# Latent attention in a two-block network: raw latents are projected, their norm becomes a column on the scores, and four heads rotate in one tile

## The reference

```python
cq, ckv, k_rope = _split(h @ w_in, (256, 128, 32))
q = (_rms_norm(cq, q_norm) @ w_uq).reshape(b, s, 16, 64 + 32)
q_nope, q_rope = q[..., :64], _rope(q[..., 64:], cos_m, sin_m)
k_rope = _rope(k_rope[:, :, None, :], cos_m, sin_m)[:, :, 0]
kv = (_rms_norm(ckv, kv_norm) @ w_ukv).reshape(b, s, 16, 64 + 64)
k_nope, v = kv[..., :64], kv[..., 64:]
sc = (q_nope . k_nope + q_rope . k_rope) * 96 ** -0.5      # causal softmax, times v, then @ w_out
```

## Time and profile before

| | us |
|---|---|
| median of 3 runs (3462.76 to 3471.7) | 3462.96 |
| profiled execution, its own time | 3462.46 |
| its span, first to last instruction | 3460.6 |
| TensorE busy | 3307.8 (96% of the span) |
| VectorE, ScalarE, GpSimd busy | 1969.4, 1264.1, 169.9 |

### The profile page before, as it was taken

One profiled execution on the slowest core, in us unless ns is written; L12 is line 12 of the kernel. 1 busy time (PEld: TensorE's weight loads), 2 busy tenths in 40 slices (PEclk: granted clock), 3 DMA queues, 4 the chain that ended last, 5 costly groups with the idle time before them and its releaser, 6 DMA issues.

```text
span 3460.6 us, 44062 instructions
## 1 busy us (share of the span) xinstructions
PE 3307.8 (96%) x16249; PEld 2737.8 (79%) x16249; DVE 1969.4 (57%) x2749; ACT 1264.1 (37%) x1953; POOL 169.9 (5%) x162
## 2 busy tenths in 40 slices
PE   7999998899999999998999999998999999889999
PEld 6888786788888788885587888898788887868887
DVE  6765534555764567555646545697555464555543
ACT  3222311454222322233344223565434343443332
POOL 0000002000000000001210000231000001000000
PEclk9999996799999999998899999999999999999999
DMA  5543233003553355322014543454333320023332
GB/s 176 169 134 97 89 98 62 1 1 105 164 154 94 94 172 164 97 81 71 7 50 135 167 123 97 128 159 137 101 97 97 101 93 25 1 73 97 97 104 67
DMA packets 389691, 344.21 MB, mean 99 GB/s; under 512 B 11392, under 2 KB 343485, under 8 KB 389565
## 3 DMA queue, kind: packets, MB, share of 16 engines
q1 hardware_dynamic: 389565, 342.52, 33.1%
HBM read 340.38 MB, written 2.10 MB: 99 GB/s over the span
## 4 chain that ended last, share of the span: by engine, by line
PE 86%; DVE 8%; ACT 3%; issue 2%; SPq 1%; POOL 0%; DMA 0%; ACTq 0%; DVEq 0%; POOLq 0%
PE ps L907 25%; PE ps L909 25%; PE ps L908 25%; PE ps L994 4%; DVE w_lo L1566 2%; PE ps L983 2%; PE ps L971 1%; ACT w_hi L1553 1%; PE ps L1157 1%; DVE rstd L2198 0%; PE ps L1139 0%; DVE q_mla L2592 0%; PE ps L1146 0%; SPq L855 0%; DVE t L2691 0%
## 5 line engine op out<-in xcount | busy, mean ns | idle before, releaser
L907 PE MATMUL ps<-a_hi,w_hi 128*128 128x512 f32 (+1 forms) x2936 | 1114.4, 380 | 43.1 <-DVE w_lo L1566 18.1
L908 PE MATMUL ps<-a_lo,w_hi 128*128 128x512 f32 (+1 forms) x2936 | 1106.9, 377 | 0.0
L909 PE MATMUL ps<-a_hi,w_lo 128*128 128x512 f32 (+1 forms) x2936 | 1106.7, 377 | 0.0
L1566 DVE TENSOR_TENSOR w_lo<-w_raw,w_hi 128x1024 fp32r<-128x1024 f32 (+1 forms) x532 | 646.2, 1238 | 249.3 <-ACT w_hi L1553 246.3
L1553 ACT ACTIVATE w_hi<-w_raw 128x1024 fp32r<-128x1024 f32 (+1 forms) x532 | 548.6, 1044 | 355.1 <-PE ps L909 345.9
L907 PEld LDWEIGHTS ps<-a_hi,w_hi 128*128 128x128 f32 x2936 | 556.5, 190 | 152.6 <-issue 39.7
L908 PEld LDWEIGHTS ps<-a_lo,w_hi 128*128 128x128 f32 x2936 | 556.7, 190 | 101.6 <-issue 2.0
L909 PEld LDWEIGHTS ps<-a_hi,w_lo 128*128 128x128 f32 x2936 | 556.0, 189 | 101.4
L907 PE MATMUL ps<-hs_hi,w_hi 128*128 128x512 f32 x1056 | 411.5, 390 | 10.6 <-DVE hs_lo L2660 10.6
L908 PE MATMUL ps<-hs_lo,w_hi 128*128 128x512 f32 x1056 | 410.9, 389 | 0.0
L909 PE MATMUL ps<-hs_hi,w_lo 128*128 128x512 f32 x1056 | 410.8, 389 | 0.0
(11 more groups left out here) (359 smaller groups left out, 3357.6 us busy)
## 6 DMA issues: line engine op xcount, KB each, us to landing
w_raw<-in_ffn_w_up SPq DMA_DIRECT2D x220, 512.0 KB, 4.8
w_raw<-in_ffn_w_down SPq DMA_DIRECT2D x154, 512.0 KB, 3.6
ada_raw<-in_ada_w SPq DMA_DIRECT2D x96, 512.0 KB, 4.0
w_raw<-in_ffn_w_gate SPq DMA_DIRECT2D x88, 512.0 KB, 4.9
w_raw<-in_ev_w_in SPq DMA_DIRECT2D x20, 512.0 KB, 3.7
w_raw<-in_attn_w_qkv SPq DMA_DIRECT2D x12, 512.0 KB, 3.8
w_raw<-in_ev_w_out SPq DMA_DIRECT2D x8, 512.0 KB, 4.3
w_raw<-in_mla_w_out SPq DMA_DIRECT2D x8, 512.0 KB, 3.6
```

Of the source, the lines that this page charges most:

```text
L907: mm(dst, hi, rhi, start=start, stop=False)
L908: mm(dst, hi, rlo, start=False, stop=False)
L909: return mm(dst, lo, rhi, start=False, stop=stop)
L1566: nc.vector.tensor_tensor(w_lo[:, s, 0:width], w_raw[:, s, 0:width], w_hi[:, s, 0:width].bitcast(F32), ALU.subtract).then_inc(lo_made.sem, 1)
```

## The change

What it does, all within this phase:

- The query latents are no longer normed. ScalarE multiplies the raw sums by the gain straight out of `ps` into `c_hi`, VectorE forms `c_lo` from `ps` too. The product of both norms' inverses, one number per token, is computed as four columns `q_rstd`, from the squares of the raw latents and the input's sum of squares, and enters as the scale of the instruction that adds the mask to the scores. The key-value latent is still normed, with one reciprocal of a sum that includes the input's.
- The last chunk of the latents is multiplied bank by bank, after the feature sum, so that the banks finish one after another.
- The weights of the queries are regrouped as they are split (`parted`): the rotary columns of four heads form one 128-column tile, plain columns of two heads another. Twelve products of six instructions replace sixteen. The keys of two heads form one tile, eight products of three instructions in place of sixteen; the values' columns lie together.
- The rotation works on `q_rope`, four heads of 32 rows in one 128-row tile: four swaps, each with three vector operations, interleaved with the projections. DMAs copy the rotated rows to the heads' `q_mla` (16 copies of 64 KB) and the rotated key to all heads (4 copies of 256 KB in place of GpSimd's copy). They stand in SyncE's queue ahead of six of the eight chunks of `w_out`. The attention waits for `rope_in`.

The diff, cut to what the prediction speaks of (removed code stands in the listing above):

```diff
-    rotation(part("mla_swap"), part("mla_cos"), part("mla_sin"), [(64, 16, pos * inverse(500000.0, 32))])
+    rotation(part("mla_swap"), part("mla_cos"), part("mla_sin"), 
+             [(first, 16, pos * inverse(500000.0, 32)) for first in range(0, P, 32)])
...
+        q_rope = arena("q_rope", [P, 4, SEQ], F32, 81920)
...
+            grouped.update({ph.first + c: (64, 32) for c in range(4, 8)})
+            grouped.update({ph.first + c: (64, 64) for c in range(8, 10)})
+            for signal in rope_in:
+                signal.plan(16 * 4)
             heads = [dict(q=(q_mla[0:96, h, :],), k=(k_mla[0:96, h, :],), v=lambda kb, h=h: v_mla[:, kb, h * HD:h * HD + HD],
-                          out=o_mla[:, :, h * HD:h * HD + HD], gate=None, need=None) for h in range(16)]
+                          out=o_mla[:, :, h * HD:h * HD + HD], gate=None, need=None, rope=rope_in[h // 4],
+                          scale=lambda c: q_rstd[:, c:c + 1]) for h in range(16)]
...
+                    for k in range(2):
+                        chunk(b + 10 + k, w["mla_w_out"][0][k * P:(k + 1) * P, :])
+                    for i in (0, 1, 2, 4, 3):
+                        sp.wait_ge(rd_s.sem, ph.rd0 + {0: 1, 1: 2, 2: 3, 4: 4, 3: 5}[i])
+                        for a in range(4):
+                            if i == 4:
+                                sp.dma_start(k_mla[64:96, 4 * a:4 * a + 4, :],
+                                             F_mla[64:96, 3, :].unsqueeze(1).to_broadcast([32, 4, SEQ])).then_inc(rope_in[i].sem, 16)
+                            else:
+                                sp.dma_start(q_mla[64:96, 4 * i + a, :], q_rope[32 * a:32 * a + 32, i, :]).then_inc(rope_in[i].sem, 16)
+                    for k in range(2, KT):
...
+                    if c == 0 and head.get("rope") is not None:
+                        pe.wait_ge(rope_in[4].sem, 16 * 4)
+                        pe.wait_ge(head["rope"].sem, 16 * 4)
...
+                    fold_ada(ph.before, 5, taken=False)
+                    w_ready(b + 3)
+                    pe.wait_ge(a_lo_s.sem, ph.al0 + KT)
+                    for t in range(4):
+                        for kk in range(2):
+                            last = latent(3, t, kk)
+                        last.then_inc(cm_s.sem if t < 3 else w_used.sem, 1)
...
+                    def query(columns, i, bank):
+                        for kk in range(2):
+                            last = three(ps[:, bank, :], columns(w_hi, i, kk), columns(w_lo, i, kk), c_hi[:, kk, :], c_lo[:, kk, :],
+                                         kk == 0, kk == 1)
+                        return last
...
+                    def query_swap(i, bank):
+                        evicted(3 * i + 1)
+                        if i == 0:
+                            pe.wait_ge(tab_s.sem, ph.tab0 + 64)
+                        mm(ps[:, bank, :], swap_mla[:, :], q_rope[:, i, :], start=True, stop=True).then_inc(rp_s.sem, 1)
...
+                    w_ready(b + 4)
+                    pe.wait_ge(a_lo_s.sem, n2.alo0 + 2)
+                    query(rope_columns, 0, 6).then_inc(cm_s.sem, 1)
+                    query(plain_columns, 0, 7).then_inc(cm_s.sem, 1)
+                    pe.wait_ge(sq_s.sem, n2.sq0 + 1)
+                    query(plain_columns, 1, 0).then_inc(w_used.sem, 1)
                     pe.wait_ge(root_s.sem, ph.root0 + 1)
...
+                    pe.wait_ge(sum_s.sem, n2.sum0 + 1)
+                    pe.wait_ge(sq_s.sem, n2.sq0 + 3)
+                    mm(ps[:, 4, :], ones[:, :], t1[:, :], start=True, stop=False)
+                    mm(ps[:, 4, :], ones[:, :], sq_sum[:, :], start=False, stop=True).then_inc(ss_s.sem, 1)
+                    pe.wait_ge(trc_s.sem, ph.before.trc0 + 1)
+                    for c in range(4):
+                        for i, part in enumerate((F_mla[:, 0, :], F_mla[:, 1, :], sq_sum[:, :])):
+                            last = mm(ps[:, 5, c:c + 1], part[:, c * P:(c + 1) * P], ones[:, 0:1], start=i == 0, stop=i == 2)
+                    last.then_inc(ss_s.sem, 1)
+                    w_ready(b + 5)
+                    query(rope_columns, 1, 1).then_inc(cm_s.sem, 1)
+                    pe.wait_ge(raw_kv_s.sem, ph.kv0 + 1)
+                    query_swap(0, 2)
...
+                    w_ready(b + 7)
+                    query(rope_columns, 3, 5).then_inc(cm_s.sem, 1)
+                    query_swap(2, 0)
+                    swapped(1)
+                    query(plain_columns, 6, 2).then_inc(cm_s.sem, 1)
+                    evicted(5)
+                    query(plain_columns, 7, 6).then_inc(w_used.sem, 1)
+                    evicted(6)
+                    mm(ps[0:96, 7, :], swap_mla[64:96, 0:96], F_mla[64:96, 3, :], start=True, stop=True).then_inc(rp_s.sem, 1)
+                    w_ready(b + 8)
                     pe.wait_ge(a_lo_s.sem, n2.alo0 + 3)
...
+                    swapped(2)
+                    key(0, 1)
+                    query_swap(3, 5)
+                    evicted(8)
+                    key(1, 3)
...
+                    evicted(12 + 8)
+                    keys_out(8)
...
+                first = grouped[n][0]
+                nc.scalar.activation(parted(w_hi, n)[1], parted(w_raw, n)[0][:, :, first:], ACT.Copy)
+                nc.scalar.activation(parted(w_hi, n)[2], parted(w_raw, n)[0][:, :, 0:first], ACT.Copy).then_inc(hi_made.sem, 1)
...
+                        do(c_hi[:, t, :], ps[:, t, :], ACT.Copy, scale=mla_gain[:, t:t + 1]).then_inc(a_hi_s.sem, 1)
...
+                        do(F_mla[:, t, :], ps[:, t, :], ACT.Square, scale=256.0 ** -0.5).then_inc(sq_s.sem, 1)
...
+                    do(t1[:, :], ps[:, 2, :], ACT.Square, scale=128.0 ** -0.5).then_inc(sq_s.sem, 1)
+                    do(F_mla[:, 2, :], ps[:, 2, :], ACT.Copy, scale=vec("mla_kv_norm")).then_inc(raw_kv_s.sem, 1)
...
+                    do(q_rstd[:, 0:4], ps[:, 5, 0:4], ACT.Sqrt, bias=eps[:, 1:2]).then_inc(root_s.sem, 1)
...
-                                           scale=at.heads[u]["scale"](c) if full else 1.0,
+                                           scale=at.heads[u]["scale"](c) if "scale" in at.heads[u] else 1.0,
...
+                    v.tensor_scalar(sq_sum[:, :], sq_sum[:, :], EPS / D_MODEL, None, ALU.mult).then_inc(sum_s.sem, 1)
...
+                        v.scalar_tensor_tensor(c_lo[:, t, :], ps[:, t, :], mla_gain[:, t:t + 1], c_hi[:, t, :].bitcast(F32),
+                                               ALU.mult, ALU.subtract).then_inc(a_lo_s.sem, 1)
...
+                    split_lo(dve, b + 8)
+                    dve.wait_ge(nrm_s.sem, n2.nrm0 + 1)
                     dve.wait_ge(tab_s.sem, ph.tab0 + 64)
...
+                    query_swapped(1, 0)
+                    query_swapped(2, 1)
+                    dve.wait_ge(a_hi_s.sem, n2.ahi0 + 3)
+                    v.tensor_tensor(c_lo[:, 2, :], F_mla[:, 2, :], c_hi[:, 2, :].bitcast(F32), ALU.subtract).then_inc(a_lo_s.sem, 1)
+                    query_roped(1, 0)
+                    split_lo(dve, b + 9)
+                    query_roped(2, 1)
+                    query_swapped(3, 2)
+                    query_roped(3, 2)
+                    dve.wait_ge(rp_s.sem, ph.rp0 + 4)
+                    dve.wait_ge(rd_s.sem, ph.rd0 + 2)
+                    v.tensor_tensor(t1[64:96, :], ps[64:96, 7, :], rope_mla[64:96, 1, :], ALU.mult).then_inc(rs_s.sem, 1)
+                    keys(0)
+                    dve.wait_ge(rs_s.sem, ph.rs0 + 4)
+                    dve.wait_ge(rc_s.sem, ph.rc0 + 4)
                     v.tensor_tensor(F_mla[64:96, 3, :], F_mla[64:96, 3, :], t1[64:96, :], ALU.add).then_inc(rd_s.sem, 1)
...
+                    query_swapped(5, 3)
+                    keys(1)
+                    keys(2)
+                    query_roped(5, 3)
+                    keys(3)
+                    split_lo(dve, b + 10)
+                    split_lo(dve, b + 11)
+                    for p in range(4, 8):
+                        keys(p)
...
+                    for r, part in enumerate((q_rope[:, 0, :], q_rope[:, 1, :], q_rope[:, 2, :], F_mla[64:96, 3, :], q_rope[:, 3, :])):
+                        rows = slice(64, 96) if r == 3 else slice(0, P)
+                        pool.wait_ge(rp_s.sem, ph.rp0 + r + 1)
+                        if r >= 3:
+                            pool.wait_ge(rc_s.sem, ph.rc0 + r)
+                        g.tensor_tensor(part, part, rope_mla[rows, 0, :], ALU.mult).then_inc(rc_s.sem, 1)```

TensorE's list from the end of the latents to the first query products. Before, the sum of the input's squares, then the sums of the latents' squares and the key's swap stand ahead of every query product:

```order
L1075 MATMUL ps<-sq_sum,ones 128x512
L1066 MATMUL ps<-ada_part,fold 32x48 x4
L1218 MATMUL ps<-sq_sum,ones 128x512
L1220 MATMUL ps<-sq_sum,ones 128x512
L1224 MATMUL ps<-F_mla,swap_mla 96x512
L907 MATMUL ps<-c_hi,w_hi 96x512
```

(48 more changed lines are left out.)

296 lines of the change are left out of this document (129 added, 167 removed).

## The result

| | kernel before | changed kernel |
|---|---|---|
| times, us | 3462.76, 3462.96, 3471.7, 3470.34, 3471.59, 3470.9 | 3442.86, 3448.26, 3443.92, 3421.63, 3414.16, 3411.0 |
| median | 3470.62 | 3432.24 |
| profiled execution | 3462.46, span 3460.6, mean clock 0.969 | 3442.86, span 3440.7, mean clock 0.965 |

The ratio is 0.9877 with an interval of 0.9835 to 0.9919: faster by 38 us (1.1%), clearly more than the 0.4% that the interval leaves to either side. But 3432 lies above the forecast of 3409 and above its range of 3402 to 3422. The six times of the changed kernel are also spread over 37 us, and the lowest three follow the mean clock of their executions: 3421.63 at 0.972, 3414.16 at 0.974, 3411.0 at 0.975, against 3443 to 3448 at 0.962 to 0.965. That is the thing to explain.

What follows compares the result with a forecast made beforehand. TensorE, carrying 86% of the chain, was taken as the bound. 53.8 us saved, less 0.3, plus 1.6, less 1.0, is 54.1; from 3462.5 that gives 3408.4, and with 0.5 for the median 3409 us, range 3402 to 3422.

Steps and rivals of the forecast that it cites:

- the two terms of the clock: TensorE's clock: 1.6 us gained at the attention's start, 1.0 us lost behind the one-column products.
- the first line of the sum: Whole kernel: the saving of 54.1 us is taken from the profiled execution's 3462.5, giving 3408.4.
- Nothing elsewhere: Outside the phase: scale column adds no instruction, attention's score groups stay at 2.21 us each head; costed at nothing.
- 54.1: Total us saved: 53.8 up to the attention's start, less 0.3 contention, plus 1.6 and less 1.0 for the clock.
- TensorE's list: TensorE's work in the new phase: sums to 59.5 us, ending at 1618.4 if nothing held it.
- VectorE's tail: VectorE's work after the key's swap: 14.8 us plus 0.2 wait, ending at 1621.5; TensorE gets a 3.1 us wait.
- Contention: Two GpSimd products behind the key's swap, meeting VectorE's work: 0.3 us for both, bounds 0 and 1.2.
- The clock: First two score groups: 3.2 us to gain at full clock, half taken, 1.6, between 0 and 3.2.
- The loss of 1.0: Behind the twelve one-column products: lower TensorE clock costs 1.0 us, between 0 and 1.7.
- DMA: Key's four copies: issue 0.43 us each, land at 1618, 4 us ahead of need; at half rate 1623, costing 1.
- The rivals: Full speed, 3403, chance 0.12; longer tail, 3415 to 3422, 0.18; crawling copies, 3480, 0.02; queries still waiting, 3422, 0.03.
- It doesn't do what it says: Queries still wait for a norm, TensorE's 13.6 us of waits stay, 40.5 saved, 3422 us; chance 0.03.

Runs made afterwards that it cites:

- changed, first repeat: The changed kernel run again unaltered: ratio 0.9865 to the kernel before, times 3412.39 to 3425.52 us.
- changed, control: The changed kernel unaltered, run beside the kernels with the filled wait: median 3415.52 us, 48.57 from feature sum to first score product.
- head by head: The changed kernel with the rotation's work done one head at a time again: 75.50 us from feature sum to first score product, 26.9 more.
- norm first: The changed kernel with the first three query products put back behind the norms: 54.66 us from feature sum to first score product, 6.1 more.
- both undone: The changed kernel with rotation per head and queries behind the norms, both at once: 80.28 us from feature sum to first score product, 31.7 more.
- shared copies: The changed kernel with ScalarE taking the second copy of the last four key pairs: 45.40 us from feature sum to first score product, median 3410.6.
- idle products: The changed kernel with four idle f32 products in TensorE's wait before the attention: first score product still 48.57 us after the feature sum, third group 2.8 to 3.1 sooner.
- splits last: The changed kernel with the two `w_out` splits behind the key copies on VectorE: 46.32 us from feature sum to first score product, 56.26 to third group.
- gap filled: The changed kernel with four small idle products in TensorE's 1.02 us wait in the untouched mixer upstream: median 3416.56 us.
- shared copies, gap filled: The changed kernel with ScalarE taking four key copies and idle products in the untouched mixer's 1.02 us wait: median 3404.94 us, ratio 0.9811 to the kernel before.

## Why the prediction was wrong

Twelve of the profiles, divided into the same three pieces by the marks above: the time up to the feature sum, from there to the third score group, and from there to the end.

| kernel | to the feature sum | to the third group | to the end | span |
|---|---|---|---|---|
| before (its sum put behind 72 products) | 1575.59 | 111.18 | 1773.83 | 3460.6 |
| changed, as first profiled | 1607.10 | 59.72 | 1773.88 | 3440.7 |
| changed, first repeat | 1576.44 | 59.97 | 1773.79 | 3410.2 |
| changed, control | 1574.42 | 59.65 | 1773.73 | 3407.8 |
| head by head | 1583.71 | 83.76 | 1774.13 | 3441.6 |
| norm first | 1602.58 | 65.70 | 1773.62 | 3441.9 |
| both undone | 1576.14 | 90.22 | 1773.84 | 3440.2 |
| shared copies | 1576.83 | 53.65 | 1773.52 | 3404.0 |
| idle products | 1575.16 | 56.83 | 1773.41 | 3405.4 |
| splits last | 1598.74 | 56.26 | 1773.80 | 3428.8 |
| gap filled | 1576.37 | 60.15 | 1773.38 | 3409.9 |
| shared copies, gap filled | 1581.34 | 53.66 | 1773.60 | 3408.6 |

The last piece agrees within 0.8 us over all of them, the middle piece within 0.5 over the four profiles in which the phase is as changed, and the first piece varies by 33 us in code that is the same in all but for the idle products of the last two.

The forecast was 3408.4 for the profiled execution, and that took 3442.86, 34.5 more. It divides into 31.5 ahead of the phase, 2.3 in the phase up to the attention, 0.3 in the two terms of the clock together, 0.1 behind it, and 0.3 around the span.

**The step that failed** is the first line of the sum, "Against the profiled execution's 3462.5", with "Nothing elsewhere": that everything outside the phase would take what it took in one profile. The cost of the change elsewhere was indeed nothing. But the base was one execution, and a favourable one. Its first piece, 1575.6, is near the best seen, 1574.4, and the kernel before has medians of 3468.3 to 3469.8 in the groups of 17 runs, 5 to 7 us above the 3463 that I took. One sign lay open: the third time shown, 3471.7, was 9 us above the other two. (The half clock that the profile before shows from 550 to 635 us was no sign, since all fourteen profiles have it there.) From 54.1, a good difference, I made an absolute time and gave it a range of only the phase's own uncertainties. Added to the kernel before's median of the long groups, the 51 us of the phase give 3418, where the changed kernel's median was 3420.85 and 3415.52 in two of them. The first median, 3432.24, lies 23.4 us above the unrounded forecast of 3408.9. Of that, 7.7 are the base (3470.62 for the kernel before in the same group, and not 3462.96), 2.6 the phase, and the remaining 13.1 are by estimate the clock upstream, since three of the six executions ran at a mean clock of 0.962 to 0.965.

**TensorE's list** of 59.5 us: right. Its last product ended 60.94 us after the first latent product, with 0.61 of waiting in it. The twelve one-column products took 2.57 (2.7 expected).

**VectorE's tail**: the wait and what ends it were right, the size 2.1 us short. From the key's swap at 1638.50 it took 17.1 us and not 15.0. The 16 copies took 11.1 us, about 0.70 from one to the next, where I had 0.61 from a row that groups eight of them in the kernel before, 9.7 in all; that is 1.4 us. Every second copy now reads the other half of the bank's partitions, and the experiment with shared copies shows that the time goes with that: there VectorE's last four copies all read the first half, and take 2.48 us together, 0.60 from one to the next. The key's rotation addition took 1.32 instead of 0.65:

```profile
1640.13 0.69 DVE L2734 COPY k_mla<-ps 64x512 f32<-64x512 f32 x1
1640.85 1.32 DVE L2754 TENSOR_TENSOR F_mla<-F_mla,t 32x512 f32<-32x512 f32 x1
...
1647.54 2.34 DVE L1680 TENSOR_TENSOR w_lo<-w_raw,w_hi 128x1024 fp32r<-128x1024 f32 x2
...
1654.87 0.69 DVE L2734 COPY k_mla<-ps 64x512 f32<-64x512 f32 x1
```

The last of these copies ends at 1655.56, and the first score product starts at 1655.66. The page calls the wait "issue", but the experiment with shared copies shows whose it is.

**Contention**: I took 0.3 in all. One meeting lengthened the tail. GpSimd's product of the next query tile ran at the same time as that addition:

```profile
1640.33 1.29 POOL L3121 TENSOR_TENSOR q_rope<-q_rope,rope_mla 128x512 f32<-128x512 f32 x1 [0.48 <-PE ps L1274]
```

They overlap from 1640.85 to 1641.62, 0.77 us, and the addition took 0.64 longer than the 0.68 that it takes in the head-by-head kernel. So most of the overlap was lost, and the 0.64 lies between my bounds of 0 and 1.2. The second meeting cost nothing: the other GpSimd product behind the key's swap, at 1638.58, ran beside a product and a copy of VectorE that read `ps`, and these took 0.69 and 0.68 as elsewhere.

**The clock** at the attention's start: I took half of the 3.2 us, and got 0.3 of it: 4.61 and 2.74 us stand in place of 4.63 and 3.01. The wait was 4.3 and not 3.4. The loss of 1.0 that I put against it behind the one-column products didn't come in this profile; the two windows behind them are at 1.00:

```profile
1622.40:1625.40 3.00, 3.00 (x12) 2.12 (x13) 2.30 (x3) 1.75 (x4) 0.52 (x1) 1.00 0.00 0
1625.40:1628.40 3.00, 3.00 (x15) 2.47 (x14) 2.44 (x3) 2.18 (x5) 0.78 (x1) 1.00 0.00 0
```

The two errors nearly cancel. That the second loss stayed away is luck. With the upstream gap filled, the same phase lost 1.6 us there, and its attention started 50.20 us after the feature sum instead of 48.6:

```profile
1590.70:1593.70 3.00, 3.00 (x16) 2.52 (x16) 2.96 (x2) 0.46 (x2) 0.00 (x0) 0.82 0.00 0
1593.70:1596.70 3.00, 3.00 (x8) 1.76 (x7) 1.83 (x4) 1.43 (x3) 1.38 (x1) 0.61 0.00 0
```

The clock fell behind them in the head-by-head kernel too (0.78 and 0.65 over 3 us each), which by the same estimate is 1.7 us of its 26.9.

**DMA**: right, though issuing the key's four copies took 3.69 us and not four times 0.43. The microsecond that a copy at half of the rate of the earlier trace rows would have cost was not in my sum, and it didn't come: the last of the four was issued from 1644.4 to 1645.9, the slowest landed 5.7 us after its issue, so all were there by 1651.6, and the first score product came at 1655.66. The page's issues give the copies' time to landing, and the attention didn't wait for them:

```profile
q_mla<-q_rope SPq DMA_DIRECT2D x16, 64.0 KB, 2.1
k_mla<-F_mla SPq DMA_DIRECT2D x4, 256.0 KB, 4.6
```

**The rivals.** None of the four happened. "It doesn't do what it says" is excluded by the rows: no wait before the queries. What did happen, a change that saves nearly what was forecast in an execution that loses 31 us elsewhere, was not among them, and of the profiled execution it took more than half of the gain away.

## What to carry to other kernels

Single executions of this kernel differ by over 30 us, more than many changes are worth, because TensorE's clock falls in some of them and not in others (from 740 to 800 us it was 0.50 in one profile of the changed kernel and 1.00 in two). Take the time of a change from a difference between two marks around the edited stage, and give an absolute forecast the spread of the unchanged kernel, which several runs show and one profile doesn't. A wait of a few us of TensorE can cost twice: 4.3 us of waiting took another 3 in the products behind it, so look for the cheapest copy to move to another engine, or fill the wait. And where product, operation and next product take turns, count both engines and the clock: the rotation head by head lengthened the phase by 26.9 us, of which 10.3 are TensorE's own products, 8.9 its waits for VectorE, and some 7.7 its lower clock.

## What was not expected of the hardware

TensorE's clock fell to half 1 to 7 us behind a wait of only 1.02 us in four profiles and not behind the same wait in seven others, two of them executions of the same program as one of the four. Once it fell with no such wait, after 13 us in which TensorE was busy for 12.87. It then stayed at 0.50 for 7 to 65 us with TensorE counted as busy throughout: 251 products in 60 us instead of 399. Copies of 64x512 f32 out of `ps` followed each other at 0.60 us where all read the same half of the partitions, and at about 0.70 where every second one read the other half. A copy of 64 KB from SBUF to SBUF landed 2.1 us after its issue, where the small table load had taken 3.0, and one that spreads 32 partitions to four heads, 256 KB, in 4.6.
